# Recurrent mixer: three waits ahead of GpSimd's differences of the fourth to sixth level

## What is computed

```python
# state space part: 8 heads, chunks of 128 tokens
seg    = exp(where(causal, a_cs[l] - a_cs[s], -inf))
y_diag = einsum('bclgn,bcsgn->bcgls', cc, bc) * seg  @ xh      # decayed scores of each head
# gated part (hgrn2): 4 heads, 128 keys each
g_cum  = cumsum(log_f)
decay  = exp(where(causal, g_cum[l] - g_cum[s], -inf))         # per key
scores = einsum('bhlk,bhlsk,bhsk->bhls', q, decay, k)
o      = o_inter + scores @ v
```

## Time and profile before

| | |
|---|---|
| median of three runs | 984.25 us |
| the profiled execution | 985.26 us |
| its span in the trace | 983.5 us |
| TensorE matmul | 97% busy |
| VectorE | 71% |
| ScalarE | 53% |
| GpSimd | 9% |
| granted TensorE clock, mean | 0.991 |

### The profile page before, as it was taken

The page is one execution under the profiler, slowest core; times in us unless marked ns, Lnnn a source line. Parts: engine busy times, 40 slices in busy tenths (PEclk is TensorE's granted clock), DMA queues, the critical chain, the costliest instruction groups (busy, mean ns, idle before and its releaser), DMA issues.

```text
span 983.5 us, 13584 instructions
## 1 busy us (share of the span) xinstructions
PE 950.1 (97%) x5540; PEld 833.6 (85%) x5540; DVE 700.8 (71%) x928; ACT 518.6 (53%) x698; POOL 88.0 (9%) x110
## 2 busy tenths in 40 slices
PE   5998999999999899899999999999999999999997
PEld 5997898888888688788988888888988799888885
DVE  4799676666667886986666666567989777666663
ACT  4796744454437646865543434368655455343442
POOL 4362000000000100000000000000132110000000
PEclk9998999999999999999999999999999999999999
DMA  9833466665555354224665656556421546656531
GB/s 321 253 119 108 133 231 194 204 201 171 187 198 178 114 168 151 87 87 139 212 206 176 209 173 203 182 151 192 151 86 44 171 129 214 214 176 209 174 126 43
DMA packets 106190, 164.40 MB, mean 167 GB/s; under 512 B 2816, under 2 KB 82784, under 8 KB 106000
## 3 DMA queue, kind: packets, MB, share of 16 engines
q1 hardware_dynamic: 104688, 158.25, 50.3%
q0 software_dynamic: 1440, 5.28, 1.5%
HBM read 162.47 MB, written 1.05 MB: 166 GB/s over the span
## 4 chain that ended last, share of the span: by engine, by line
PE 73%; DVE 16%; ACT 4%; issue 3%; DMA 2%; POOL 1%; DVEq 0%; ACTq 0%; POOLq 0%
PE ps L379 71%; DVE wl L1748 5%; DVE SC L1862 2%; PE ps L387 2%; DMA raw<-in_w_in 1%; ACT junk L1166 1%; DVE xf L1769 1%; ACT wh L1178 1%; DVE xhl L1765 1%; ACT SC L1499 1%; DVE rows L2369 1%; ACT xhl L1184 1%; POOL st L2533 1%; DVE st L2160 0%; DVE hs L1780 0%
## 5 line engine op out<-in xcount | busy, mean ns | idle before, releaser
L1748 DVE TENSOR_TENSOR wl<-raw,wh 128x2048 fp32r<-128x2048 f32 (+2 forms) x149 | 337.3, 2266 | 148.8 <-ACT wh L1178 148.4
L1178 ACT ACTIVATE wh<-raw 128x2048 fp32r<-128x2048 f32 (+2 forms) x150 | 282.1, 1886 | 158.4 <-PE ps L379 141.5
L379 PE MATMUL ps<-xhl,wh 128*128 128x512 f32 (+1 forms) x1248 | 256.1, 352 | 2.5 <-ACT wh L1243 2.5
L379 PEld LDWEIGHTS ps<-xhl,wh 128*128 128x128 f32 x1248 | 200.8, 191 | 29.8 <-issue 3.6
L379 PE MATMUL ps<-wh,xhl 128*128 128x512 f32 (+3 forms) x1000 | 195.4, 339 | 2.9 <-ACT SC L1441 1.8
L379 PEld LDWEIGHTS ps<-wh,xhl 128*128 128x128 f32 x1000 | 155.2, 190 | 21.7 <-ACT SC L1441 2.2
L379 PEld LDWEIGHTS ps<-xhl,wl 128*128 128x128 f32 x1008 | 135.6, 191 | 7.5
L379 PE MATMUL ps<-xhl,wl 128*128 128x256 f32 x1008 | 140.6, 282 | 0.0
L379 PE MATMUL ps<-wl,xhl 128*128 128x512 f32 (+3 forms) x500 | 105.3, 336 | 0.1
L379 PE MATMUL ps<-wh,fh 128*128 128x512 f32 x304 | 91.2, 392 | 1.0 <-DVE fl L2006 0.7
L379 PE MATMUL ps<-wh,fl 128*128 128x512 f32 x304 | 90.4, 390 | 0.0
(11 more groups left out here) (271 smaller groups left out, 844.2 us busy)
## 6 DMA issues: line engine op xcount, KB each, us to landing
raw<-in_ffn_gate SPq DMA_DIRECT2D x22, 1024.0 KB, 5.4
raw<-in_ffn_up SPq DMA_DIRECT2D x22, 1024.0 KB, 5.5
raw<-in_ffn_down SPq DMA_DIRECT2D x22, 1024.0 KB, 4.9
raw<-in_w_up SPq DMA_DIRECT2D x16, 1024.0 KB, 5.6
raw<-in_w_down SPq DMA_DIRECT2D x16, 1024.0 KB, 5.0
raw<-in_s_w_in SPq DMA_DIRECT2D x14, 1024.0 KB, 5.4
raw<-in_w_in SPq DMA_DIRECT2D x9, 1024.0 KB, 7.5
raw<-in_a_w_in SPq DMA_DIRECT2D x6, 1024.0 KB, 5.1
```

The source lines that it names most:

```text
L379: return e.matmul(o, a, b, start=start, stop=stop, skip_group_check=True)
L1178: e.activation(high_of(i), raw_of(i), ACT.Copy).then_inc(*up("act_high", i))
L1748: e.tensor_tensor(low_of(i), raw_of(i), high_of(i).bitcast(F32), ALU.subtract).then_inc(*up("dve_lo", i))
```

## The change

GpSimd waits before part(4) until VectorE has made the decayed scores of head 3, before part(5) of head 5, and before part(6) of head 7. The waits that the parts have themselves stay. Part(7) gets no wait of its own and stands behind part(6). Nothing else is changed.

```diff
@@ -2610,8 +2610,11 @@
             part(1)
             part(2)
             part(3)
+            e.wait_ge(*at("dve_decayed", 3))
             part(4)
+            e.wait_ge(*at("dve_decayed", 5))
             part(5)
+            e.wait_ge(*at("dve_decayed", 7))
             part(6)
             part(7)
             for tb in range(2):
```

## The result

| | median | runs | lowest to highest |
|---|---|---|---|
| before | 984.88 us | 20 | 983.63 to 985.60 |
| after | 986.35 us | 20 | 985.40 to 987.67 |

The ratio after to before is 1.0017, with a 95% interval of 1.0011 to 1.0023: the change makes the kernel slower by 1.1 to 2.3 us. The time is at the upper edge of my range (986.4), where I had put a case of 0.12. One execution of the kernel after_part7_later took 2323.4 us where its other ten took 983.97 to 985.88 (the weight loads of one line took 378 ns each where before has 191); it is left out of the ratio, and that kernel's rows come from another execution, part7_later_again.

The account below looks back on a forecast made before the run. It took TensorE to bound the kernel and VectorE the stage from 744.65 us. TensorE's 0.72 us turn into waits and VectorE ends 0.73 us later: about +0.7 on 984.25 gives 984.95 us, range 983.3 to 986.4.

Parts of the forecast that it names:

- What bounds the stage: From 744.65 to 763 us VectorE runs without notable pause and releases gated(0); a shift there arrives whole at the end.
- The price of a halt: A VectorE instruction with two SBUF inputs halted by a GpSimd difference; 0.80 us for a weighing at part(4).
- TensorE's gain of 0.72 us: TensorE's wait for decayed(2) at 734.65 us goes, so seg(7) and decay(5) come 0.72 us earlier.
- Part(4): GpSimd gets in after weigh(3)'s first instruction and delays the second by 0.80 us; its own second falls beside masked scores.
- GpSimd waits for whole weigh pairs: Stated sign that the prediction is wrong: GpSimd kept out through both instructions of a weighing.
- The premise that they take turns: Whichever of GpSimd and VectorE is first is served to nearly its end, then they alternate, even with VectorE's queue full.
- Part(5): At weigh(4), GpSimd's start at 739.01 and VectorE's at 739.06 called a tie; VectorE taken as first, one 0.80 us halt.
- the forecast's +0.73 us: At weigh(5) the second weighing ends at 746.68 instead of 745.95, so L1748 also ends 0.73 us later.
- Part(6) and part(7): GpSimd starts ahead of weigh(5), whose second weighing ends 0.73 us later; part(7) then costs L1748 the same 0.80 us.
- GpSimd first at part(5) too: Rival: GpSimd wins the tie, both weigh(4) instructions are halted, weigh(6)'s first is 1.1 us late: 985.35 us; chance 0.25.
- the gain stays: Rival: VectorE's two weighings keep GpSimd out, weigh(5) ends 0.8 us earlier, 0.25 us remains: 984.0 us; chance 0.16.
- slower, by turns: Rival: GpSimd halts both instructions at every weighing and late decays hold up the next; seven halts, +2.2: 986.4 us; chance 0.12.

Follow-up runs that it names:

- after_part7_later: The kernel after, with part(7) behind one more wait, for weigh(6); ratio to before 0.9998 (0.9988 to 1.0007).
- part7_later_again: Same kernel as after_part7_later, executed again for a readable profile; stage 37.22 us against 38.05 in after.
- one_later: The kernel before, with part(4) to part(7) each waiting for weigh(n-1) in place of weigh(n-2); ratio to before 0.9994, stage 36.67 us.
- after_part5_later: The kernel after, with a small GpSimd memset (some 0.2 us) between the wait for decayed(5) and part(5); ratio to before 1.0001, stage 37.37 us.
- w5_only: The kernel before plus only the wait ahead of part(5), for decayed(5); ratio to before 1.0015, stage 38.07 us.
- w6_only: The kernel before plus only the wait ahead of part(6), for decayed(7); ratio to before 1.0018, stage 38.21 us.

## Why the prediction was off

- **What bounds the stage**: right. The shift at gated(0) is the shift at the end.
- **The price of a halt**: right in size (0.80 us forecast, 0.60 to 1.08 measured). The 0.19 us by which a halted instruction ends before the plain sum was read at the decayed scores; at the weighings after the change it is 0.13 to 0.14 us (751.31+0.68-751.85 for weigh(6)).
- **TensorE's gain of 0.72 us**: the wait is gone, as forecast, but it was worth nothing by itself; one_later shows that the stage follows VectorE's sum even so. In after TensorE waits 1.43 us ahead of state_turn(0) instead, one of the places that the prediction named, and 0.25 us ahead of level(4).
- **Part(4)**: right sum, wrong place. GpSimd took 2.03 us and stood back through both weighings, and its second instruction halted decayed(4) by 0.68 us. I had it get in after the first weighing, by the one row of decayed(1). "GpSimd waits for whole weigh pairs" was my own sign of a wrong prediction, and it came true at weigh(3) and weigh(5). The premise that they take turns doesn't hold in general. At part(4) that changed the place of a halt and not its price.
- **Part(5)**: this is the step that failed. I called it a tie and gave it to VectorE, on the ground that a separate wait costs GpSimd time. The separate wait cost nothing that the rows show: decayed(5) ended at 739.26 and part(5) started 0.08 us later, decay(4) ended at 739.25 and weigh(4) started 0.10 us later, so that GpSimd was first by 0.01 us. My own sum had it first by 0.05 us (739.01 against 739.06). One halt of 0.80 became two, 1.97 us together, after decayed(4) had already been halted. In after_part5_later, where the tie goes to VectorE, the forecast's +0.73 us is what the stage shows.
- **Part(6) and part(7)**: three halts behind decayed(7), as counted, but in other places. Since VectorE was late, it was first at weigh(5), lost nothing there, and was 0.28 us ahead of before at the end of L1748 (750.41 against 750.22+0.47). Part(7) came so late that both its instructions hit weigh(6), 1.68 us.
- **The rival "GpSimd first at part(5) too"** is what happened. Its +1.1 us was too low since it let GpSimd into weigh(5) once and so had part(7) earlier, with one halt in weigh(6), where the stage shows +1.41 us. I gave it 0.25 where a tie deserved as much as the forecast.
- **The rival "the gain stays"**: its condition, that two weighings keep GpSimd out, held at weigh(3) and weigh(5), but not at weigh(4), where GpSimd was first; so there was no gain.
- **The rival "slower, by turns"**: its 986.4 is within 0.1 us of the measured time by luck. It took seven halts or more and +2.2 us on a base of 984.25; there are six, +1.4 to +1.5 us on a base of 984.88, and ScalarE's decays hold up weigh(4) alone, by 0.17 us.
- **The base**: I put the shift on the median of three runs, 984.25; over twenty it is 984.88. That is 0.6 us of the 1.4 by which my time is low.

## To carry to other kernels

Before moving work of GpSimd by a wait, look at what VectorE runs right behind the release: an instruction with one input in PSUM can cover it, one with two inputs in SBUF is halted, here by 0.60 to 1.08 us for a subtraction of 1.04. In w5_only, w6_only and after_part5_later VectorE was waiting for ScalarE's decay when the decayed scores released GpSimd, and GpSimd went first. When forecast times of two engines tie within 0.1 us, give both orders the same chance and follow each to the end; here one order cost 0.7 us and the other 1.4.

## What the runs showed of the hardware that I had not expected

GpSimd, asking 0.13 to 0.16 us after VectorE's instruction had begun, was let in ahead of VectorE's next one in two places and stood back through a second one in others (2.03 us for a subtraction of 1.04). A satisfied wait between VectorE's two instructions did not change that. The rule behind it is open.
